# Dealing the context pieces between the expert steps by work instead of by number

## The reference, cut to what matters

```python
hid = (jax.nn.silu(t @ w_gate[g, e]) * (t @ w_up[g, e]) * combine)
out = out + hid @ w_down[g, e]        # w_gate, w_up: 1024 x 512, w_down: 512 x 1024
```

```python
hc = rmsnorm(ctx, g_pre) * (1 + scale_c) + shift_c
u = hc @ w_in                          # q, k, v, o, z, pool and gate columns
h, state = mlstm_chunkwise(q, k, v, log_i, log_f, zero)   # 4 heads, 2 directions, 2 chunks of 128
y = concat(headnorm(h * sigmoid(o)) * silu(z), pool(u) * silu(pg)) @ w_out
ctx = ctx + gate_c * rmsnorm(y, g_post)
```

## Time and profile before

| what | value |
|---|---|
| median of 3 runs | 1731.17 us (1726.09 to 1734.52) |
| the profiled execution | 1726.63 us, span from the first to the last instruction 1724.8 us |
| PE busy | 1557.5 us (90%) |
| mean granted PE clock | 0.94 of full speed |
| read from memory | 389.80 MB |
| expert stage, first step to last step | 540.0 us to 1130.3 us |

### The profile page before, as it was taken

One profiled execution on the slowest core, in us unless ns is written; L12 is line 12 of the kernel. 1 busy time (PEld: TensorE's weight loads), 2 busy tenths in 40 slices (PEclk: granted clock), 3 DMA queues, 4 the chain that ended last, 5 costly groups with the idle time before them and its releaser, 6 DMA issues.

```text
span 1724.8 us, 22009 instructions
## 1 busy us (share of the span) xinstructions
PE 1557.5 (90%) x9293; PEld 1069.7 (62%) x9293; DVE 487.9 (28%) x1221; ACT 340.9 (20%) x706; POOL 4.1 (0%) x8
## 2 busy tenths in 40 slices
PE   6999979899979879988998999976889989999997
PEld 3655678778865433643364754555676776888666
DVE  2200164451134321222114100024343322022481
ACT  2310150212021112011210000023112032021461
POOL 0000000000000000000000000000000000000000
PEclk8999996799979889999999999986999999999998
DMA  9989530122148998999999999941313223323100
GB/s 378 421 350 377 201 130 1 49 101 98 49 189 339 379 410 361 412 395 408 416 395 418 402 407 423 374 185 38 146 49 139 105 98 126 135 93 147 49 2 25
DMA packets 54303, 397.57 MB, mean 230 GB/s; under 512 B 6359, under 2 KB 13688, under 8 KB 16440
## 3 DMA queue, kind: packets, MB, share of 16 engines
q1 hardware_dynamic: 40384, 341.85, 49.4%
q10 hardware_dynamic: 13240, 52.16, 7.6%
q0 software_dynamic: 576, 2.10, 0.4%
HBM read 389.80 MB, written 6.29 MB: 230 GB/s over the span
## 4 chain that ended last, share of the span: by engine, by line
PE 77%; DMA 9%; DVE 5%; ACT 4%; issue 2%; SPq 1%; PEld 1%; ACTq 0%; PEldq 0%; DVEq 0%
PE bank L680 15%; PE bank L1417 12%; PE bank L1432 8%; PE bank L2346 6%; DMA work<-in_moe_w_up 4%; PE bank L2363 4%; PE bank L1532 3%; PE bank L1537 3%; PE bank L525 2%; PE bank L2332 2%; DMA work<-in_moe_w_gate 2%; PE bank L711 2%; DMA work<-in_ada_w 2%; PE bank L1140 2%; PE bank L1128 2%
## 5 line engine op out<-in xcount | busy, mean ns | idle before, releaser
L680 PE MATMUL bank<-H,ring 128*128 128x256 f32 (+1 forms) x960 | 244.7, 413 | 6.1 <-ACT work L1057 4.0
L680 PEld LDWEIGHTS bank<-H,ring 128*128 128x128 f32 x960 | 183.0, 192 | 59.7 <-issue 34.2
L2346 PE MATMUL bank<-ring,work 128*32 128x512 f32 (+1 forms) x768 | 137.4, 626 | 17.3 <-DMA work<-in_moe_w_gate 6.3
L1417 PE MATMUL bank<-H,work 128*128 128x256 f32 x512 | 114.1, 381 | 0.1
L1417 PE MATMUL bank<-H,ring 128*128 128x256 f32 x512 | 112.9, 381 | 0.0
L1417 PEld LDWEIGHTS bank<-H,work 128*128 128x128 f32 x512 | 96.0, 190 | 18.7 <-issue 6.2
L1417 PEld LDWEIGHTS bank<-H,ring 128*128 128x128 f32 x512 | 98.1, 192 | 13.6
L2346 PEld LDWEIGHTS bank<-ring,work 128*32 128x32 f32 (+1 forms) x768 | 36.5, 121 | 105.2 <-issue 83.4
L1432 PE MATMUL bank<-work,H 128*128 128x512 f32 x192 | 85.2, 596 | 0.0
L1432 PE MATMUL bank<-ring,H 128*128 128x512 f32 x192 | 83.0, 592 | 0.0
L2363 PE MATMUL bank<-ring,work 128*32 128x512 f32 (+1 forms) x384 | 67.5, 618 | 2.8 <-issue 2.2
(11 more groups left out here) (410 smaller groups left out, 1989.3 us busy)
## 6 DMA issues: line engine op xcount, KB each, us to landing
ring<-in_moe_w_gate SPq DMA_DIRECT2D x48, 1024.0 KB, 10.4
ring<-in_moe_w_up SPq DMA_DIRECT2D x48, 1024.0 KB, 9.0
ring<-in_moe_w_down SPq DMA_DIRECT2D x48, 1024.0 KB, 11.7
work<-in_ab_w_in ACTq DMA_DIRECT2D x28, 1024.0 KB, 10.1
ring<-in_ab_w_in SPq DMA_DIRECT2D x14, 2048.0 KB, 7.5
work<-in_ada_w SPq DMA_DIRECT2D x12, 2048.0 KB, 15.6
ring<-in_w_in SPq DMA_DIRECT2D x12, 2048.0 KB, 9.6
work<-in_w_mod SPq DMA_DIRECT2D x12, 2048.0 KB, 8.9
```

The costliest lines, as they stand in the source:

```text
L680: mm = nc.tensor.matmul(bank[i % NB][:, 0:n], weight(c, k, j * P, (j + 1) * P), rhs(k), start=(k == 0), stop=(k == kt - 1))
L1417: mm = nc.tensor.matmul(b[:, j * T:(j + 1) * T], w_k(m, n, k, at, at + P), H[:, k, m.s], start=(k == 0), stop=(k == DT - 1), skip_group_ch ...
L2346: mm = nc.tensor.matmul(bank[b][rows, :], gath[:, k, rows], half_slot[(load_at[n + half] + e) % NHALF][:, (k % 4) * 512:(k % 4 + 1) * 512] ...
```

## The change

The numbers of pieces are no longer written down. Each piece gets a work figure (`BODY`: 8 for half a tile, 5, 1, 2 or 3 for a memory piece, 4 for a pooling piece, 2 for a light one, 0 for an empty one), each pass gets a share (91 for a pass of four, 12 for a pass of two), each share is spread over the nine points (1 each, 0.5 for the last two), and `spread` takes pieces until the share due so far is met. Nothing else changes: the pieces, their order, and the order around them on each engine are the same.

```diff
-        FILL_FOUR, FILL_TWO = (2, 2, 2, 2, 2, 2, 2, 1, 1), (0, 0, 0, 1, 0, 1, 0, 0, 0)
+        TILE, LIGHT = 8, 2
+        MEMORY = (5,) + (1, 2) * 2 + (3, 2) * 2
+        HEADS_OUT = MEMORY * 2 + (TILE,) * 8 + (LIGHT,)
+        BODY = ((TILE,) * 4 + (LIGHT,) + HEADS_OUT + (TILE,) * 12 + HEADS_OUT + (TILE,) * 8 + (0,) + (4,) * NPOOL + (TILE,) * 8 + (TILE,) * 16)
+        SHARE = (1, 1, 1, 1, 1, 1, 1, 0.5, 0.5)
+        PASS_SHARE = [91 if experts == 4 else 12 for _, experts in PASSES]
+
+        def spread(work):
+
+            table, at, spent, due = [], 0, 0.0, 0.0
+            for share in PASS_SHARE:
+                row = []
+                for part in SHARE:
+                    due += share * part / sum(SHARE)
+                    n = 0
+                    while at < len(work) and spent + work[at] / 2 <= due:
+                        spent += work[at]
+                        at += 1
+                        n += 1
+                    row.append(n)
+                table.append(tuple(row))
+            return table
+
+        FILL = spread(BODY)
 
         def fill(body, p, i):
 
-            for _ in range((FILL_FOUR if PASSES[p][1] == 4 else FILL_TWO)[i]):
+            for _ in range(FILL[p][i]):
                 next(body, None)
```

## The result

The changed kernel takes 1768.92 us (median of 4, 1763.09 to 1772.52) against 1730.01 us (median of 4, 1726.09 to 1734.52): ratio 1.0229, interval 1.0203 to 1.0255. The direction was forecast. The size was not: +38.9 us instead of +14.8, and 1768.9 lies above the forecast's range, which ended at 1764. The profiled execution took 1763.09 us, its span is 1761.3 us, 36.5 longer than before.

A forecast was written before the change was run, and what follows sets the result against it. The expert stage was taken as bound by the DMA stream and PE, each delaying the other. Standstill of 29 + 15 + 4 + 6 = 54 us, 27 more, less 12.1 at the end, gave +14.9: 1746 us, range 1722 to 1764.

The forecast's parts named there:

- The walk: Step-by-step account of passes 0 to 3, claiming DMA standstill of 29 us in passes 0 and 1, 15 in 2 and 3.
- pass 1: Expert stage, pass 1: 2.5 us of standstill added where a head's output waits for DVE.
- a half tile in pass 9: End of the stage: this half tile's PE lateness and its cover were counted inside the 12.1 us saved.
- up to step 4: Pass 0: step 3 ends about 575.5 us, step 4 at 604 instead of 594.1; 15 us of standstill.
- the second crowd: Memory pieces at points 5 to 8 of pass 2 and point 0 of pass 3: 15 us of standstill.
- the 4 us of the clock: Two more slow steps behind crowded points, where PE is late, cost 4 us (bounds 0 and 8).
- passes 0 and 1: Start of the expert stage: five or six memory pieces in a row make DMA stand still 29 us in sum.
- The rival in which a piece costs its units: Whole stage: waits of DVE and ACT hide, standstill falls, kernel 12 us faster at 1719 us; chance 0.15.
- The rival in which the lead absorbs part: Crowds with the clock cost 34 us of standstill, not 48; +1 us, 1732 us; chance 0.23.
- the row numbers: Pass 0: DVE starts them behind the first five memory pieces, costing PE a 3.9 us wait.
- what is saved at the end: Behind the stream: last step and three half tiles take 14.2 us where before 26.3 lay, saving 12.1 us.
- Two signs that failed: PE waiting for DVE at L1485 and L1496 over 20 us, twice before; last step starting as its halves land.

The follow-up runs named there:

- a: The changed kernel with the pieces of passes 0 and 1 spread about two to a point: 1741.69 us, ratio 1.0080 to the kernel before.
- b: The changed kernel with the 22 pieces of pass 2 spread two or three to a point: 1749.26 us, ratio 1.0133 to the kernel before.
- g: The kernel before with passes 0 and 1 dealt as in the changed kernel and fewer pieces in pass 2: 1752.35 us, ratio 1.0139.
- f: The changed kernel with memory pieces' work figures from traced durations and share 104 for passes of four: 1740.28 us, ratio 1.0081 to the kernel before.
- c: The changed kernel with DVE computing the row numbers in pass 5 instead of pass 0: 1760.95 us, ratio 1.0182 to the kernel before.
- e: The changed kernel with passes 0, 1 and 2 spread evenly and row numbers in pass 5: 1724.83 us, ratio 0.9980 to the kernel before.
- i to l: Four variants of the kernel before, three half tiles more in pass 3, differing in piece placement or row numbers' pass: ratios 1.0039, 1.0071, 1.0069, 1.0068.
- h: The kernel before with only the row numbers moved from pass 0 to pass 5: 1723.45 us, ratio 0.9965.
- d: The changed kernel with passes 6 to 9 dealt as in the kernel before: 1770.87 us, ratio 1.0231 to the kernel before.

## Why the prediction was right in direction and short in size

**In short.** Two terms of the sum failed. The walk gave pass 1 a standstill of 2.5 us, and it had 10.1. And a half tile in pass 9 that I called covered was not, so that the end saved 7.2 us instead of 12.1. The other differences are smaller: 3.3 us more up to step 4, 3.7 more in the second crowd, the 4 us of the clock (they have no row of their own in what was measured), and 5.7 us behind the last half tile.

**Right: what bounds the kernel, and the mechanism.** The bytes are the same, the stream's end moved by what DMA stood still (from 1118 to 1156 us, 38, against 37.5 by the table above), and DMA stands still where PE is late to a step. The holes stand at the forecast places: 225 and 194 GB/s from 580 to 620 us, 111 GB/s at 800 to 820. Runs a, b and g show the new tables of passes 0 and 1 and of pass 2 to be the cause, each by itself. (a and g change passes 0 and 1 together, so no run prices pass 1 alone.) The rival in which a piece costs its units is refuted by g and f: the same pieces with the trace's durations as their figures lose less than half as much. The rival in which the lead absorbs part had 34 us of standstill in the two crowds; 58.1 were measured, and in g the light pass 2 gave back 3.3 us of 27. The Trainium skill has the general case in "Perfetto Trace Analysis", section Optimization Strategy: where the most-contended engine changes over time, interleaving the regimes may help. The trace agrees in the reverse direction: memory pieces were interleaved with steps, and the first crowd, which puts them together, cost 1.39%.

**Short: passes 0 and 1, 29 us forecast (31 with their share of the clock term), 39.4 measured. The step that failed is pass 1.** Three windows of the changed kernel divide the stretch:

```profile
579.00:609.00 30.00, 24.45 (x117) 15.68 (x116) 15.00 (x49) 4.84 (x12) 0.00 (x0) 0.77 0.40 164
609.00:641.40 32.40, 27.72 (x129) 13.79 (x129) 11.35 (x32) 7.42 (x14) 0.00 (x0) 0.89 0.71 276
641.40:720.00 78.60, 67.83 (x360) 35.60 (x360) 12.10 (x26) 12.35 (x22) 0.00 (x0) 0.93 0.90 366
```

- Up to step 4: 15 us of standstill forecast, 18.3 measured. The 3 us are the one event at the start of the walk. "Steps 0 to 3 come out as before" gave 575.5 for the end of step 3, and it ended at 578.7. PE had waited 3.97 us for ACT at the gate columns (568.11 above), since at point 2 these pieces now follow a half tile, with no step to hide ACT's part. Step 3 still started on time, but from the wait on the matmuls ran slow, 24 of step 3's 32 among them (1.07 us for two of them instead of 0.60). From there the walk nearly kept its lengths: 30.3 us instead of 28.5 to the end of step 4, then 17.2 for 16.5 and 15.2 for 16.0 (step 4 ended at 609.0 instead of 604, step 5 at 626.2 instead of 620.5, step 6 at 641.4 instead of 636.5).
- Steps 5 and 6: 11.5 us forecast, 11.1 measured.
- Pass 1: 2.5 us forecast ("where a head's output waits for DVE"), 10.1 measured. These 7.6 us are most of the 10.4 between 29 and 39.4. It is no crowd of memory pieces: step 9 ends at 675.4, and step 10 only at 699.7, 24.3 us later where the lead is 20:

```profile
675.45 3.84 PE L2355 MATMUL bank<-work 128*128 128x128 f32 x32
...
689.90 1.41 PE L1505 MATMUL bank<-ident,work 128*128 128x128 f32 x8 [3.31 <-DVE work L1864]
...
696.06 3.64 PE L2386 MATMUL bank<-ring,work 128*32 128x512 f32 x32
```

The wait of 3.31 us for DVE is the one that I had priced, but gather, three half tiles, the head's output and the wait stand in one row between the two steps, and step 9 itself had waited 7.46 us for its halves, so at 675.4 the stream was not a full lead ahead. From 684 to 700 us it moved 240 GB/s. Before, that pass had already lost 6.1 us (640 to 690), and the walk names nothing that would have saved more than half of it.

Of the row numbers the 3.9 us forecast are there: c is 3.6 us shorter from the gather to step 4.

**Not borne out: where the clock costs.** I put 4 us on steps behind the crowds, by the 5.57 us of the earlier trace rows. Those steps ran at full speed: 3.64 us at 605.33, and 3.64 at 810.64. The loss is inside the crowd and at step 3 instead. At a granted clock of 0.79 and 0.76 part of the memory matmuls ran at 1.2 GHz, 2.01 us for four of L1496 (590.94) where 1.14 is full speed (814.21). Over the whole program the same 9293 matmuls kept PE busy for 1574.2 us instead of 1557.5; how much of these 16.7 us reached the stream no run separates, so whether 4 us was near the right size stays open. The Trainium skill's rule, "TensorE: Matmul & The Clock Gate", section Why this matters for your kernels, names idle gaps as what brings the clock down; the trace agrees for step 3, which ran slow behind the gap of 3.97 us. Inside the crowd the single gaps were 0.3 to 2.3 us, and the clock fell too, in a stretch in which PE was busy 14.92 of 20 us.

**Nearly right: the second crowd,** 15 to 17 us forecast, 18.7 measured. Both steps that I named are the late ones: step 17 ends at 788 and step 18 starts at 810.64, 22.6 us apart, against 19 us of pieces forecast.

**Wrong: what is saved at the end, 12.1 us forecast.** The stream ended at 1156 us (the last halves issued at 1144.64, 11.4 us to land), and the last half tile ended at 1175.1: 19.1 us behind it, where I had 14.2 and before had 26.3. So 7.2 us are saved. PE's last rows show it:

```profile
1157.18 3.73 PE L1532 MATMUL bank<-work 128*128 128x256 f32 x16
1160.84 3.65 PE L2386 MATMUL bank<-work 128*64 128x512 f32 x16
1164.42 3.73 PE L1532 MATMUL bank<-work 128*128 128x256 f32 x16
1168.00 7.07 PE L1537 MATMUL bank<-H,work 128*128 128x256 f32 x32
```

A half tile at point 5 of pass 9 stands between the two last steps, so the last step starts at 1160.84, 5 us after its halves landed. I had called that half tile covered; these 5 us are what is missing in the saving.

**Not foreseen:** 3 us in the tail (below), and 2.7 us in the rest of the program, which I can't place. The sum: 38 us of stream, 7.2 us saved at the end, which makes 30.8 us at the last half tile, 3 and 2.7 more: 36.5 us of span.

**Two signs that failed.** DVE's waits at L1485 and L1496 are 18.5 us, not over 20 and not twice those of before. That sign was badly chosen: what cost the time was the length of the row of pieces between two steps, clock included, not the sum of their waits. And the last step did not start as its halves landed, but 5 us later.

**One loose reading.** "Nowhere else does it stay there" overlooks the first four slices, at 350 to 421 GB/s; nothing in the sum uses it.

## What to carry to other kernels

Where a stream runs a fixed lead ahead of the engine that uses it up, what may not grow is the time between two of that engine's steps beyond that lead (here two steps of bytes, 8.4 MB or 20 us at 420 GB/s). Everything between the two steps counts, the gather and a wait included; spreading equal work over passes says nothing of that. Count a piece by the time until the next one can start, as the trace shows it at the place where it will stand, not by its matmuls: with such figures the same dealing out lost 0.8% and not 2.3%. And look at what stands fixed beside the pieces that move: the row numbers of DVE, moved alone, were worth 0.35% in the kernel before, while no table tried beat that.

## What the runs showed of the hardware that was not expected

**A wait of ACT that ends behind POOL's gathers.** In the tail ACT loads a table at L1270 and computes a square root. In the changed kernel 2.96 us pass between them, with a queue named that the profile does not know; before, none. Of the changed kernel:

```profile
1174.69 1.07 POOL L2344 DMA_INDIRECT work<-expert_rows,work  x1 [1174.23 <-DMA expert_rows<-work]
...
1176.25 1.28 ACT L1270 ACT_TABLE_LOAD   x1
...
1178.55 0.94 POOL L2344 DMA_INDIRECT work<-expert_rows,work  x1 [0.30 <-issue]
1180.50 0.31 ACT L1270 ACTIVATE rstd<-bank,epsc 128x64 f32<-128x64 f32 x1 [2.96 <-remote]
```

In five of the 14 traces (the changed kernel, a, b, c, e) the load starts 1.1 to 1.6 us behind the start of the first of four gathers, and the square root waits 2.96 to 3.48 us for that queue. In f it starts half a us before the last gather, and 1.3 us pass, for which the profile names PE. In i to l it starts 0.1 to 0.3 us ahead of the first gather, in the kernel before, g and h behind the last, in d well ahead: no wait at this place. But d shows that the table load is not needed for it: its next square root, with no load ahead of it, waits 2.65 us for the same queue while the gathers run. What these seven have in common is the end: the square root starts 0.9 to 1.2 us behind the end of the last gather. In i to l a square root starts in the midst of the gathers without a wait. The cause stays open; no run put this to the test by itself.

**The rate of the stream.** One core kept 416 to 419 GB/s through windows of 40 to 140 us (g and h), with halves of a megabyte. The rows of before had shown 408 GB/s over 371 us.
